# Expert blocks of 32 tokens in four column groups, with ten weight places, in a two-block transformer kernel

## The chip, the cores and the metric

The kernel runs on one core of a Trainium2 chip, as one program. The metric is the device time of one execution in microseconds; the kernel before was run three times.

## The reference

Two stacks of layers on 256 tokens of 1024 features, all in fp32. The first stack has two layers (latent attention, then a short convolution), each followed by a mixture of experts; the second has two layers of feed-forward, mixer, feed-forward. The part that matters here:

```python
def _hier_moe(h, w_group, b_group, w_expert, b_expert, w_gate, w_up, w_down):
    g_prob = softmax(h @ w_group)                       # 4 groups
    g_sel = argmax(g_prob + b_group)
    e_prob = softmax((h @ w_expert) of the chosen group) # 8 experts
    top_idx = top_k(e_prob + e_bias, 2)
    top_w = normalised e_prob[top_idx] * g_prob[g_sel]
    ...
    expert(x, e) = (silu(x @ w_gate[e]) * (x @ w_up[e])) @ w_down[e]
    return sum over the token's two experts of top_w * expert(token)
```

There are 32 experts. w_gate[e] and w_up[e] are 1024 x 512, w_down[e] is 512 x 1024, so each is one piece of 2 MB and an expert has 6 MB. Which tokens an expert gets is known only at run time.

## The kernel before

**Stages.** The engines run one list of stages: an opening, attention, norm, experts of layer 0, norm, convolution, norm, experts of layer 1, norm, and then a loop over the two layers of the second stack. The expert stage is the class `Moe`; it runs twice, on 256 tokens.

**Router.** TensorE forms the router's logits (L1480) and turns the tokens into rows (L1488), which ScalarE keeps (L1616) and writes to `f_rows` in HBM (L1619). VectorE picks each token's two experts in small steps. Tokens of an expert are put in blocks of `CAP` = 64. The number of blocks of an expert is one plus the number of multiples of `CAP` that its count exceeds (L1734 to L1737), and a token's block and place follow from its rank in the same way (L1748 to L1753). A table says for each block which tokens it has and with what weights (L1510, L1766 to L1770); it is done when `table_kept` is signalled. The first block number of each expert is in `FIRSTI`, and each engine reads its loop's limits from there (`range_of`). An expert has at least one block.

**One block**, in TensorE's order (`expert` in `Moe.pe`): gate (L1557) and up (L1558), 64 tokens as the stationary operand and 512 weight columns moving, gate in array columns 0 to 63 and up in 64 to 127, for eight slices of the 1024 features; then the next block's tokens are turned (`turn_block`, L1530); then the block before is combined (L1523); then the hidden rows are turned (L1574), and down (L1581, L1582) follows, again in two halves. An fp32 matmul shows as two records in the trace. Beside it ScalarE does SiLU (L1642), keeps the next tokens (L1633) and the down result (L1648); VectorE multiplies (L1780), keeps the turned hidden rows (L1783) and builds the combine matrix (L1787); GpSimd gathers the tokens of the block after the next from `f_rows` (L1820, L1823), as 128 half rows of 2 KB.

**Weights.** A piece of weights lives in a place of 16 KB a partition: six places in `ring` and three in `arena`, so nine, and experts e, e+1, e+2 hold three each (`AHEAD` = 3). SyncE issues all weight loads from one queue, in order. Ahead of the expert stage it issues the six loads into the ring as the stage before frees them, then three into the arena once the norm is done (L2911). When the table is there, a loop (L2947) issues for each expert e, in order, gate and up of expert e+3 when the last `hidden` of expert e is signalled, and down of e+3 when its last `down` is (L2944):

```python
for j, name in enumerate(("moe_w_gate", "moe_w_up", "moe_w_down")):
    freed = moe.hidden if j < 2 else moe.down
    sp.wait_ge(freed.sem, blocks)
```

Behind the loop it waits for the blocks of expert 30, and goes on with the next stage's loads (L2911). Such a load waits until the piece that was last in its ring place is used: for a piece of expert 31 that is the end of the last combine. Expert 31 has three ring places. In the second expert stage these are places 0, 1 and 2, which the first feed-forward loads want.

Other lines that are named: the conditioning matmuls of the opening (L452), the norm's sums (L724) and square root (L746), and the rounding of feed-forward weights on ScalarE (L2100).

Of the kernel before, what the change touches and what calls it, by code (L numbers as in the profile page):

```python
# [44 lines left out]
CAP = P // 2  # L45
# [17 lines left out]
AHEAD = (RING + EXTRA) // 3  # L63
# [125 lines left out]
def program(nc, xT, vec, base_c, mla_c, mix_c, w, out):  # L189
    ctx = ExitStack()  # L190
    with ctx:
# [69 lines left out]
        slot_in = [sig(f"slot_in{i}") for i in range(RING + EXTRA)]  # L261
# [1096 lines left out]
        class Moe:  # L1358
# [5 lines left out]
            def __init__(self, l, tokens, norm):  # L1364
# [36 lines left out]
                places = [(self.first + i) % RING for i in range(RING)] + [RING + i for i in range(EXTRA)]  # L1401
                for e in range(EXPERTS):

                    done = (self.down, 0) if e < EXPERTS - 1 else (self.combined, 2)
                    for j, (name, shape) in enumerate((("moe_w_gate", (2, 4 * FF)), ("moe_w_up", (2, 4 * FF)), ("moe_w_down", (1, FT * D)))):
                        plan(self.rows_of(name, w[name][l][e]), shape, done, places[3 * (e % AHEAD) + j])
# [29 lines left out]
                self.XG = take(512)  # L1436
                self.YS = take(512)

                rows_at = take.used()
                self.SG, self.H = take(FF), take(FF)  # L1440
                self.XB = take(512).rearrange("p (c a) -> p c a", c=4)
# [3 lines left out]
                assert rows_at + 2 * D == take.used() <= EXTRA_AT, (rows_at, take.used())  # L1445

            def rows_of(self, name, weight):

                if name == "moe_w_down":
                    return weight.rearrange("(o p c) n -> p o (c n)", o=1, p=P)  # L1450
                return weight.rearrange("(j p c) n -> p j (c n)", j=2, p=P)

            def weights(self, a, which):

                wv = slot(self.first + 3 * a + which)
                if which == 2:
                    return wv.rearrange("p (c n) -> p c n", c=FT)
                return wv.rearrange("p (j c n) -> p j c n", j=2, c=4)

            def arrived(self, eng, turn, a, which):  # L1460

                n = self.first + 3 * a + which
                eng.wait_ge(slot_in[place_of[n]].sem, turn * 16 + arrivals[n])
                eng.sem_inc(spare.sem, 1)

            ADDED = (0, 1, 4, 5, 2, 3, 6, 7)

            def combined_tile(self, k):

                return ps[:, (1, 4, 5, 6)[k // 2], k % 2 * TL:(k % 2 + 1) * TL]  # L1470

# [1606 lines left out]
```

## Time and profile before

| | |
|---|---|
| runs | 2464.44, 2465.23, 2462.46 us; median 2464.44 |
| profiled execution | 2464.74 us, its span 2462.9 us |
| mean granted TensorE clock | 0.980 of full speed |
| busy, share of the span | TensorE 95%, weight loads 66%, VectorE 46%, ScalarE 35%, GpSimd 4% |
| HBM | 677.87 MB read, 277 GB/s over the span |
| MB by weight loads of the expert stages | 192 loads of 2048 KB |

The two loops over the experts' blocks take 470 and 456 us of the span. Busy time of TensorE is that of records whose ends are modelled, so that it says little about how fast the records follow each other; for that their starts are read.

### The profile page before, as it was taken

To read this page: it belongs to the slowest core of one execution; us is meant where nothing else is said; L and a number is where in the kernel's file an instruction comes from. 1 tells how busy PE (TensorE), PEld (TensorE's weight loads), DVE (VectorE), ACT (ScalarE), POOL (GpSimd) and SP (SyncE) were. 2 spreads that over 40 slices of the span, in tenths; PEclk is the share of its full clock that TensorE was granted. 3 is DMA by queue.
4 is the path that set the end of the run, shared out by engine and by line. 5 is a ranking of instruction groups with operands and counts; after the bars stand their busy time and mean duration, and the time that the engine had idled before them with its cause. 6 is when DMAs were issued, how large, how long until landed. Compare 5 with 4: busy or idle time off the path is not lost.

```text
span 2462.9 us, 37675 instructions
## 1 busy us (share of the span) xinstructions
PE 2329.7 (95%) x13114; PEld 1621.6 (66%) x13117; DVE 1136.7 (46%) x2043; ACT 853.6 (35%) x1521; POOL 109.6 (4%) x180
## 2 busy tenths in 40 slices
PE   7999899999999989999999999998999999998997
PEld 3567444444447944444444688886888788886886
DVE  4676311111115641111111676776666766767666
ACT  2232111111114421111111555554554654554554
POOL 0000000000000000000000000000000000000000
PEclk8999899999999999999999999999999999999999
DMA  9974798999997549999998755435446456334552
GB/s 390 334 277 190 314 425 368 428 427 426 428 394 280 197 185 425 428 427 427 427 428 373 272 169 167 144 104 171 167 143 220 150 162 193 130 120 138 174 155 82
DMA packets 295807, 668.84 MB, mean 272 GB/s; under 512 B 10596, under 2 KB 205156, under 8 KB 254208
## 3 DMA queue, kind: packets, MB, share of 16 engines
q1 hardware_dynamic: 289440, 658.82, 69.4%
q0 software_dynamic: 5520, 4.23, 0.5%
q10 hardware_dynamic: 720, 4.13, 0.4%
q8 instruction: 76, 1.25, 0.2%
q14 instruction: 51, 0.42, 0.0%
HBM read 677.87 MB, written 3.15 MB: 277 GB/s over the span
## 4 chain that ended last, share of the span: by engine, by line
PE 87%; DVE 5%; DMA 3%; issue 2%; ACT 1%; SPq 1%; ACTq 0%; DVEq 0%; POOLq 0%; POOL 0%; PEldq 0%
PE ps L2120 19%; PE ps L1557 16%; PE ps L2125 10%; PE ps L1581 8%; PE ps L1523 5%; PE ps L2394 4%; PE ps L2559 2%; PE ps L1530 2%; DMA ring<-in_moe_w_up 2%; PE ps L1558 1%; PE ps L1923 1%; PE ps L1924 1%; PE ps L1925 1%; DVE arena L1783 1%; PE ps L1574 1%
## 5 line engine op out<-in xcount | busy, mean ns | idle before, releaser
L2120 PE MATMUL ps<-XS,WS 128*128 128x512 f32 x1408 | 500.4, 400 | 12.5 <-DVE XS L679 11.8
L2105 DVE TENSOR_TENSOR WS<-ring,WS 128x1024 fp32r<-128x1024 f32 (+1 forms) x276 | 329.5, 1194 | 229.8 <-ACT WS L2100 229.3
L2100 ACT CAST WS<-ring 128x1024 fp32r<-128x1024 f32 (+1 forms) x276 | 283.0, 1026 | 333.4 <-PE ps L2125 312.3
L2125 PE MATMUL ps<-XS,WS 128*128 128x256 f32 x1408 | 397.1, 282 | 0.0
L1780 DVE TENSOR_TENSOR arena<-arena,ps 64x512 f32<-64x512 f32 x65 | 44.8, 690 | 712.2 <-ACT arena L1642 712.2
L1557 PE MATMUL ps<-ring,arena 128*64 128x512 f32 x720 | 319.1, 597 | 5.1 <-issue 2.0
L2120 PEld LDWEIGHTS ps<-XS,WS 128*128 128x128 f32 x1408 | 265.7, 189 | 83.4 <-DVE XS L679 22.7
L1558 PE MATMUL ps<-ring,arena 128*64 128x512 f32 x720 | 319.3, 597 | 0.0
L2125 PEld LDWEIGHTS ps<-XS,WS 128*128 128x128 f32 x1408 | 268.6, 191 | 0.0
L1557 PEld LDWEIGHTS ps<-ring,arena 128*64 128x64 f32 x720 | 98.8, 138 | 192.6 <-issue 192.6
L2120 PE MATMUL ps<-HS,WS 128*128 128x512 f32 x616 | 216.7, 397 | 0.0
L2125 PE MATMUL ps<-HS,WS 128*128 128x256 f32 x704 | 197.7, 281 | 0.0
L1581 PE MATMUL ps<-ring,arena 128*64 128x512 f32 x360 | 162.8, 595 | 27.4 <-DVE arena L1783 27.4
L1648 ACT COPY arena<-ps 128x512 f32<-128x512 f32 x65 | 38.0, 585 | 390.9 <-PE ps L1582 390.9
L1642 ACT ACTIVATE arena<-ps 64x512 f32<-64x512 f32 x65 | 38.3, 589 | 367.2 <-PE ps L1558 367.2
L1582 PE MATMUL ps<-ring,arena 128*64 128x512 f32 x360 | 164.1, 599 | 0.0
L1557 PE MATMUL ps<-arena 128*64 128x512 f32 x320 | 140.6, 592 | 0.7 <-DMA arena<-in_moe_w_up 0.7
L1558 PE MATMUL ps<-arena 128*64 128x512 f32 x320 | 140.6, 593 | 0.0
L1523 PE MATMUL ps<-arena 64*128 64x256 f32 x1072 | 133.9, 389 | 1.8 <-ACT arena L1648 1.8
L2125 PEld LDWEIGHTS ps<-HS,WS 128*128 128x128 f32 x704 | 133.4, 190 | 0.1
L2120 PEld LDWEIGHTS ps<-HS,WS 128*128 128x128 f32 x616 | 115.6, 188 | 27.1
L1581 PEld LDWEIGHTS ps<-ring,arena 128*64 128x64 f32 x360 | 45.6, 136 | 101.5 <-issue 101.5
(361 smaller groups left out, 3668.7 us busy)
## 6 DMA issues: line engine op xcount, KB each, us to landing
ring<-in_ffn_w_gu SPq DMA_DIRECT2D x90, 1024.0 KB, 7.3
ring<-in_moe_w_gate SPq DMA_DIRECT2D x44, 2048.0 KB, 16.8
ring<-in_moe_w_up SPq DMA_DIRECT2D x44, 2048.0 KB, 21.5
ring<-in_moe_w_down SPq DMA_DIRECT2D x44, 2048.0 KB, 19.6
ring<-in_w_mod SPq DMA_DIRECT2D x24, 2048.0 KB, 10.2
ring<-in_ffn_w_down SPq DMA_DIRECT2D x32, 1408.0 KB, 6.5
arena<-in_moe_w_gate SPq DMA_DIRECT2D x20, 2048.0 KB, 17.2
arena<-in_moe_w_up SPq DMA_DIRECT2D x20, 2048.0 KB, 21.9
```

Of the source, the lines that this page charges most:

```text
L1523: mm = pe.matmul(self.combined_tile(4 * half + i), self.YS[rows, i * P:(i + 1) * P], self.COMBINE[rows, :], start=False, stop=last and i % ...
L1530: mm = pe.transpose(ps[:, 3, c * P:(c + 1) * P], by_four[:, c, :], IDENT)
L1557: pe.matmul(ps[0:CAP, 0, :], x, gate[:, j, c, :], start=k == 0, stop=k == KD - 1)
L1558: mm = pe.matmul(ps[CAP:P, 0, :], x, up[:, j, c, :], start=k == 0, stop=k == KD - 1)
L1581: pe.matmul(ps[0:CAP, 7, :], self.HB[:, c, :], down[:, c, 0:512], start=c == 0, stop=c == FT - 1)
L1582: mm = pe.matmul(ps[CAP:P, 7, :], self.HB[:, c, :], down[:, c, 512:D], start=c == 0, stop=c == FT - 1)
L2100: L.inc(L.eng.copy(self.parts(u)[0], source), self.w_high)
L2105: L.inc(L.eng.tensor_tensor(wl, self.unit(u)[1], high(wh), ALU.subtract), self.w_split)
L2120: L.eng.matmul(ps[:, bank, :].rearrange("p (j t) -> p j t", j=2), wh[:, i, :], moving[:, :, k, :], start=k == 0, stop=False)
L2125: mm = L.eng.matmul(ps[:, bank, 0:TL], wl[:, i, :], moving[:, 0, k, :], start=False, stop=k == total - 1)
L2394: mm = pe.matmul(out_ap, weights[:, k, :], XS[:, x, k, :], start=k == 0 and x == 0 and weights is high_part, stop=k == KD - 1 and weights ...
L2559: mm = pe.matmul(self.y_tile(m), weights[:, k - first, cols], YS[:, k, x, :], start=m % 2 == 0 and k == 0 and x == 0 and weights is high_part,
```

## The change

- `CAP` is 32. A block's gate and up are four products side by side in the array, each with 32 tokens stationary and 256 weight columns moving: gate in two halves, up in two halves, in array columns 0, 32, 64 and 96. Down is four quarters of 256 columns, and the combine uses the four groups of 32 rows. SiLU, the multiply and the copies work on 256 columns; the turned hidden rows are copied in two parts.
- The arithmetic for blocks and places uses one comparison with all multiples of `CAP` and a sum, in place of a step for each multiple. The count uses 2 columns in place of 128. The memset of the gathered rows is moved behind the rows' writes and ahead of the wait for the table.
- Tokens are gathered as 32 whole rows of 4 KB.
- All three kinds of weights are loaded as one row of 16 KB a partition (gate and up were two rows of 8 KB each).
- The tenth place is the memory `A` of the normed tokens, which is free once the tokens' rows are turned. Gate and up have four places each (two in the ring and two elsewhere), down has two, both in the ring. So gate and up of expert e+4 are loaded when expert e has used its own, down of e+2 when e has used its own. The last experts hold other ring places than before: expert 31 has one ring place only, its down.

```diff
-CAP = P // 2
+CAP = P // 4
+HALF_FF = FF // 2
-AHEAD = (RING + EXTRA) // 3
+AHEAD, DOWN_AHEAD = 4, 2
+A_PLACE = RING + EXTRA
...
+            if at == A_PLACE:
+                return A[:, :, :].rearrange("p k n -> p (k n)")
...
+                near = [(self.first + i) % RING for i in range(RING)]
+                far = [RING + i for i in range(EXTRA)] + [A_PLACE]
+                places = {"moe_w_gate": (near[0], near[3], far[0], far[2]), "moe_w_up": (near[1], near[4], far[1], far[3]),
+                          "moe_w_down": (near[2], near[5])}
...
                         for k in range(KD):
-                            c, j = k // 2, k % 2
-                            x = self.XB[:, c, j * CAP:(j + 1) * CAP]
-                            pe.matmul(ps[0:CAP, 0, :], x, gate[:, j, c, :], start=k == 0, stop=k == KD - 1)
-                            mm = pe.matmul(ps[CAP:P, 0, :], x, up[:, j, c, :], start=k == 0, stop=k == KD - 1)
+                            x = self.XB[:, k, :]
+                            for q in range(4):
+                                weight = (gate, up)[q // 2][:, k, q % 2 * HALF_FF:(q % 2 + 1) * HALF_FF]
+                                mm = pe.matmul(ps[self.lane_rows(q), 0, 0:HALF_FF], x, weight, start=k == 0, stop=k == KD - 1)
...
-                        pe.wait_ge(self.h_kept.sem, b + 1)
+                        pe.wait_ge(self.h_kept.sem, b * 2 + 2)
                         pe.sem_inc(spare.sem, 1)
                         for c in range(FT):
-                            pe.matmul(ps[0:CAP, 7, :], self.HB[:, c, :], down[:, c, 0:512], start=c == 0, stop=c == FT - 1)
-                            mm = pe.matmul(ps[CAP:P, 7, :], self.HB[:, c, :], down[:, c, 512:D], start=c == 0, stop=c == FT - 1)
+                            for q in range(4):
+                                mm = pe.matmul(ps[self.lane_rows(q), 7, 0:D // 4], self.HB[:, c, :],
+                                               down[:, c, q * (D // 4):(q + 1) * (D // 4)], start=c == 0, stop=c == FT - 1)
...
-                step(v.tensor_copy(self.CNT[0:EXPERTS, :], ps[0:EXPERTS, 6, 0:P]))
-                step(v.tensor_scalar(self.NBLK[0:EXPERTS, :], self.CNT[0:EXPERTS, :], float(CAP), 1.0, ALU.is_gt, ALU.add))
-                for r in range(2, -(-self.T // CAP)):
-                    step(v.scalar_tensor_tensor(out=self.NBLK[0:EXPERTS, :], in0=self.CNT[0:EXPERTS, :], scalar=float(r * CAP),
-                                                in1=self.NBLK[0:EXPERTS, :], op0=ALU.is_gt, op1=ALU.add))
+                over = self.CNT[0:EXPERTS, 0:limits]
+                step(v.tensor_tensor(over, self.LIMITS[0:EXPERTS], ps[0:EXPERTS, 6, 0:1].to_broadcast([EXPERTS, limits]), ALU.is_lt))
+                step(v.tensor_reduce(self.CNT[0:EXPERTS, limits:limits + 1], over, X, ALU.add))
+                step(v.tensor_scalar(self.NBLK[0:EXPERTS, :], ONES[0:EXPERTS, :], self.CNT[0:EXPERTS, limits:limits + 1], 1.0,
+                                     ALU.mult, ALU.add))
...
-                for i in range(EXTRA):
-                    load(n + i)
-                n += EXTRA
+                for e, j in ((2, 0), (2, 1), (3, 0)):
+                    load(moe.first + 3 * e + j)
+
+                sp.wait_ge(moe.rows_turned.sem, moe.rows_turned.base + moe.NT)
+                load(moe.first + 3 * 3 + 1)
...
+                    kinds = (("moe_w_gate", AHEAD, moe.hidden), ("moe_w_up", AHEAD, moe.hidden), ("moe_w_down", DOWN_AHEAD, moe.down))
+                    for j, (name, ahead, freed) in enumerate(kinds):
+                        if j == 2 or gate_too:
+                            sp.wait_ge(freed.sem, blocks)
+                            at = moe.first + 3 * a + j
+                            src = w[name][moe.l][bass.ds(e + ahead, 1)].rearrange("o (p c) n -> p o (c n)", p=P)
+                            sp.dma_start(loads[at][0][0], src).then_inc(slot_in[place_of[at]].sem, 16)
```

In SyncE's queue the loads ahead of the first expert stage's loop, and the loop's first expert, stand like this before (`gate`, `up` and `down` name the weights, the text ahead of the arrow the memory that is written; an ISA row is a wait):

```order
L2911 DMA arena<-in_moe_w_gate 128x2x2048
L2911 DMA arena<-in_moe_w_up 128x2x2048
L2911 DMA arena<-in_moe_w_down 128x4096
L2947 UNCONDITIONAL_BRANCH
L2947 ISA
L2931 TENSOR_LOAD arena
L2931 ISA x2
L2944 ISA
L2944 DMA ring<-in_moe_w_gate 128x2x2048
L2944 DMA ring<-in_moe_w_up 128x2x2048
L2944 DMA ring<-in_moe_w_down 128x4096
```

and with the change like this:

```order
L2925 DMA arena<-in_moe_w_gate 128x4096
L2925 DMA arena<-in_moe_w_up 128x4096
L2925 DMA arena<-in_moe_w_gate 128x4096
L2925 DMA A<-in_moe_w_up 128x4096
L2960 UNCONDITIONAL_BRANCH
L2960 ISA
L2947 TENSOR_LOAD arena
L2947 ISA x2
L2958 ISA
L2958 DMA ring<-in_moe_w_gate 128x4096
L2958 DMA ring<-in_moe_w_up 128x4096
L2958 ISA
```

The third piece ahead of the loop is now gate of expert 3, not down of expert 2, and a fourth goes to `A`; the down load follows behind a wait of its own.

On TensorE the end of a block's gate and up (L1557, L1558) and what follows it stand like this before:

```order
L1557 MATMUL ps<-ring,arena 64x512
L1558 MATMUL ps<-ring,arena 64x512
L1561 ISA
L1530 MATMUL ps<-BASE,arena 128x128 x4
L1523 MATMUL ps<-arena 128x256 x8
L1574 MATMUL ps<-BASE,arena 128x64 x4
```

and the whole block like this with the change:

```order
L1566 MATMUL ps<-ring,arena 32x256 x32
L1569 ISA
L1538 MATMUL ps<-BASE,arena 128x32 x8
L1531 MATMUL ps<-arena 128x256 x8
L1582 MATMUL ps<-BASE,arena 64x64 x4
L1467 ISA
L1587 ISA
L1591 MATMUL ps<-ring,arena 32x256 x16
```

The order of the block's parts is unchanged; gate and up are 32 matmuls of half the columns instead of 16, and down 16 instead of 8.

## Rows read from the trace of the kernel before

**Rows 1.** The page, part 5 (costliest groups; its heading gives the columns).
```profile
L1780 DVE TENSOR_TENSOR arena<-arena,ps 64x512 f32<-64x512 f32 x65 | 44.8, 690 | 712.2 <-ACT arena L1642 712.2
```
**Rows 2.** Stretches: us; busy time of PE, PEld, DVE, ACT, POOL; clock, DMA share, GB/s.
```profile
960.00:1320.00 360.00, 343.14 (x1822) 168.35 (x1820) 42.46 (x100) 54.84 (x84) 30.13 (x50) 1.00 1.01 427
282.00:288.00 6.00, 5.97 (x16) 2.10 (x18) 0.00 (x0) 1.28 (x1) 0.67 (x1) 0.55 0.05 10
396.00:400.00 4.00, 4.00 (x20) 1.55 (x18) 0.00 (x0) 0.58 (x1) 0.00 (x0) 1.00 0.64 269
400.00:404.00 4.00, 4.00 (x22) 1.68 (x20) 0.00 (x0) 0.00 (x0) 0.00 (x0) 1.00 0.01 4
404.00:408.00 4.00, 3.95 (x30) 2.69 (x26) 0.70 (x2) 1.18 (x2) 1.21 (x2) 1.00 0.44 123
```
**Rows 3.** Timeline, one block of the first expert stage: start, us taken, engine, instruction.
```profile
602.88 0.75 PE L1530 MATMUL ps<-BASE,arena 128*128 128x128 f32 x4
603.56 2.00 PE L1523 MATMUL ps<-arena 64*128 64x256 f32 x16
...
606.00 0.43 DVE L1783 COPY arena<-ps 128x256 f32<-128x256 f32 x1 [1.70 <-PE ps L1574]
...
606.58 0.61 PE L1581 MATMUL ps<-ring,arena 128*64 128x512 f32 x1 [0.61 <-DVE arena L1783]
...
610.03 0.59 PE L1557 MATMUL ps<-ring,arena 128*64 128x512 f32 x1
...
610.46 0.59 PE L1557 MATMUL ps<-ring,arena 128*64 128x512 f32 x1
...
617.03 0.75 PE L1530 MATMUL ps<-BASE,arena 128*128 128x128 f32 x4
```
**Rows 4.** Timeline, TensorE: the first gate record of either stage.
```profile
282.02 1.08 PE L1557 MATMUL ps<-ring,arena 128*64 128x512 f32 x1 [1.57 <-ACT arena L1633]
...
905.56 0.61 PE L1557 MATMUL ps<-ring,arena 128*64 128x512 f32 x1 [1.72 <-issue]
```
**Rows 5.** Timeline, SyncE's queue: gate loads in the expert loops.
```profile
291.97 0.40 SPq L2944 DMA_DIRECT2D ring<-in_moe_w_gate  x1
...
376.82 0.38 SPq L2944 DMA_DIRECT2D ring<-in_moe_w_gate  x1
...
405.11 0.37 SPq L2944 DMA_DIRECT2D ring<-in_moe_w_gate  x1
...
912.86 0.38 SPq L2944 DMA_DIRECT2D ring<-in_moe_w_gate  x1
```
**Rows 6.** Stretches in which the last weights of either stage arrive.
```profile
730.00:735.00 5.00, 4.39 (x32) 3.23 (x32) 1.70 (x4) 1.18 (x2) 1.20 (x2) 1.00 0.69 287
1345.00:1350.00 5.00, 4.76 (x24) 1.78 (x22) 0.00 (x0) 0.58 (x1) 0.00 (x0) 1.00 0.42 179
```
**Rows 7.** Timeline: the last down record of either stage, and what follows the second.
```profile
751.08 0.59 PE L1582 MATMUL ps<-ring,arena 128*64 128x512 f32 x1
...
1361.40 0.59 PE L1582 MATMUL ps<-ring,arena 128*64 128x512 f32 x1
...
1364.94 33.14 SPq L2911 DMA_DIRECT2D ring<-in_ffn_w_gu  x12
1365.07 3.72 PE L724 MATMUL ps<-A,BASE 128*128 128x256 f32 x16 [0.16 <-ACT A L703]
...
1373.01 1.99 ACT L2100 CAST WS<-ring 128x1024 fp32r<-128x1024 f32 x2 [5.25 <-DMA ring<-in_ffn_w_gu]
...
1376.31 0.42 ACT L746 ACTIVATE RS<-RS 128x256 f32<-128x256 f32 x1
```
**Rows 8.** Timeline, opening: weight loads of 128 rows by 32 columns.
```profile
22.37 0.13 PEld L452 LDWEIGHTS ps<-ring,arena 128*32 128x32 f32 x4 [0.30 <-issue]
...
22.80 0.13 PEld L452 LDWEIGHTS ps<-ring,arena 128*32 128x32 f32 x4 [0.30 <-issue]
```
**Rows 9.** Timeline, VectorE: a counting step of the router.
```profile
259.89 0.59 DVE L1737 SCALAR_TENSOR_TENSOR arena<-arena 32x128 f32<-32x128 f32 x2
```

More of the change, by code:

```diff
@@ L260, in program @@
         stages_done = sig("stages_done")
-        slot_in = [sig(f"slot_in{i}") for i in range(RING + EXTRA)]
+        slot_in = [sig(f"slot_in{i}") for i in range(A_PLACE + 1)]
         spare = sig("spare")
@@ L1444, in __init__, with rows_of, lane_rows @@
                 self.ROWS = [arena[:, rows_at + i * D:rows_at + (i + 1) * D] for i in range(2)]
[L1445 to L1451, printed above, removed]
+                assert rows_at + 2 * D <= take.used() <= EXTRA_AT, (rows_at, take.used())
+            def rows_of(self, weight):
+                return weight.rearrange("(o p c) n -> p o (c n)", o=1, p=P)
             def weights(self, a, which):
[L1455 to L1458, printed above, removed]
+                return slot(self.first + 3 * a + which).rearrange("p (c n) -> p c n", c=FT if which == 2 else KD)
             def arrived(self, eng, turn, a, which):
                 n = self.first + 3 * a + which
-                eng.wait_ge(slot_in[place_of[n]].sem, turn * 16 + arrivals[n])
+                per_turn = 16 * (AHEAD // DOWN_AHEAD if which == 2 else 1)
+                eng.wait_ge(slot_in[place_of[n]].sem, turn * per_turn + arrivals[n])
                 eng.sem_inc(spare.sem, 1)
-            ADDED = (0, 1, 4, 5, 2, 3, 6, 7)
+            ADDED = tuple(range(KD))
             def combined_tile(self, k):
                 return ps[:, (1, 4, 5, 6)[k // 2], k % 2 * TL:(k % 2 + 1) * TL]
+            def lane_rows(self, q):
+                return slice(q * CAP, (q + 1) * CAP)
             def pe(self, L):
@@ L1513, in pe @@
                 L.inc(mm, self.table)
[L1515 to L1516 removed]
+                by_eight = self.XG[0:CAP].rearrange("p (n c) -> p c n", c=KD)
+                hidden_by_four = self.H[0:2 * CAP].rearrange("p (n c) -> p c n", c=FT)
                 def combine(last=False):
[L1520 to L1526 removed]
+                    for i in range(2):
+                        for q in range(4):
+                            rows = self.lane_rows(q)
+                            mm = pe.matmul(self.combined_tile(2 * q + i), self.YS[rows, i * P:(i + 1) * P], self.COMBINE[rows, :],
+                                           start=False, stop=last and i == 1)
+                            if last and i == 1 and q % 2 == 1:
+                                L.inc(mm, self.combined)
                 def turn_block():
[L1529 to L1530 removed]
+                    for c in range(KD):
+                        mm = pe.transpose(ps[:, 3, c * CAP:(c + 1) * CAP], by_eight[:, c, :], IDENT[0:CAP, 0:CAP])
                     mm.then_inc(self.block_turned.sem, 1)
@@ L1747, in dve @@
                     pick(self.BLK[c], row(self.FIRST[:, 0:EXPERTS], EXPERTS), self.O32[c], EXPERTS)
-                    step(v.tensor_scalar(self.QUOT[c], self.RANK[c], float(CAP), None, ALU.is_ge))
-                    for r in range(2, -(-self.T // CAP)):
-                        step(v.scalar_tensor_tensor(out=self.QUOT[c], in0=self.RANK[c], scalar=float(r * CAP), in1=self.QUOT[c],
-                                                    op0=ALU.is_ge, op1=ALU.add))
+                    over = self.TMP[:, :, 0:limits]
+                    step(v.tensor_tensor(over, lanes(self.RANK[c], limits), row(self.LIMITS, limits), ALU.is_ge))
+                    step(v.tensor_reduce(self.QUOT[c][:, :, 0], over, X, ALU.add))
                     step(v.tensor_tensor(self.BLK[c], self.BLK[c], self.QUOT[c], ALU.add))
```

84 lines of the change are left out of this document (35 added, 49 removed).

## The prediction

> **What bounds the kernel now.** I read the page first, then each expert stage by stretches, then one block in order of time, then SyncE's queue, and last the two ends of a stage. The page counts 65 trips of the block loop (x65), 33 in the first expert stage and 32 in the second [rows 1]. The stretches show two limits side by side: from 960 to 1320 us TensorE is busy 343 of 360 us at clock 1.00, and the DMA engines are busy all the time (share 1.01) at 427 GB/s [rows 2]. Which of the two ends last is read from the block. From one block's token transposes (602.88) to the next's (617.03) it is 14.15 us: 16 pairs of gate and up records, 6.86 us at 0.4286 a pair; 3.70 us from the transposes to the first down matmul; 8 pairs of down, 3.43 us; a seam of 0.15 [rows 3]. So TensorE needs 14.14 us a block, and the two stages take 282.0 to 751.7 and 905.6 to 1362.0 [rows 3, 4, 7].
>
> The DMA side: an expert's three pieces are 2.097 MB each. In the second stage the first load in the loop is issued at 912.86 [rows 5], its first bytes come some 2 us later, and the last of 87 pieces is in at 1347.1, since the stretch 1345 to 1350 still moves data for 42% of its time [rows 6]: 432.2 / 87 = 4.97 us a piece, 14.9 an expert. The first stage gives the same: 294.0 to 733.4, less 7.7 us without traffic between 396 and 408 (36%, 99% and 56% of three stretches of 4 us), is 431.7 / 87 = 4.96 [rows 2, 5, 6]. That gap is the one expert with two blocks: one expert's gate load is issued at 376.82, the next one's only at 405.11. So the stages are almost balanced: TensorE paces them at 14.14, DMA could do no better than 14.9 and lives on nine pieces loaded beforehand, which are used up just at the end.
>
> **The change, part by part.**
>
> *How many blocks.* I worked the router out from the reference with its inputs. Blocks of 64 give 33 and 32, as the trace has. Blocks of 32 give 36 and 34: in the first layer experts 0, 7 and 25 get 34, 74 and 38 tokens (2, 3 and 2 blocks), in the second experts 4 and 27 get 60 and 48 (2 each). 70 blocks instead of 65.
>
> *One block.* Gate and up are now four column groups of 32 with 256 columns each. Whether four groups run together is shown at the start of this kernel, where a conditioning matmul uses exactly that form: four weight loads of 128x32 begin together, and the next four 0.43 us later (22.37, 22.80), with 512 columns each [rows 8]. A group of four records so takes what a pair takes now, and with 256 columns half of it, 0.214. Gate and up have 16 such groups, 3.43 us, and down 8, 1.72. The middle part stays near 3.7: eight transposes of 32 rows in place of four of 128 (bounds: 0.68 us as now, to twice that, taken 1.2), the combine with four row groups instead of two (2.00 us as now, to half, taken 1.1), SiLU and multiply on half the columns (hidden below both), and two copies in place of one of 0.43 before down (between none and 0.5 more, taken 0.3) [rows 3]. Sum: 3.43 + 3.7 + 1.72 + 0.1 = 8.95 us a block, bounds 8.3 and 10. An expert with one block then needs 9 us of TensorE and 14.9 of DMA: **the stage becomes DMA bound**, and only 1 us of TensorE speed in many shows.
>
> *The loads.* They can be spared nothing in bytes. Rows of 16 KB for gate and up: down has such rows already in the same stream and the stream stands at 427 GB/s; bounds 0 and 2% faster, taken 0.3%, 4.95 us a piece. The tenth place takes one more piece before the loop, so 86 remain: 425.7 us a stage. The Trainium skill (DMA: Bandwidth & Descriptors, "Where 436 GB/s comes from") puts the ceiling at 435 GB/s; at that rate a piece would take 4.82 us and the two stages would give 22 us more. No row here holds more than 427 over a long stretch.
>
> *First stage.* The router's shorter counting (two steps in place of the 0.59 us of L1737 and two more, twice again for the ranks, a count of 2 columns instead of 128) and a memset taken off the path give 1.5 us (0 to 3) [rows 9], so the loop starts at 280.5. The first block runs at half clock as now (0.55 from 282 to 288) [rows 2], 3 us extra. Expert 0 has two blocks, so its gate is free at 280.5 + 6.4 + 5.5 + 3.5 = 295.9; 2.3 us later data flow, at 298.2; plus 425.7 is 723.9. Expert 7 with three blocks holds its places until the four deep gate and up queue is nearly dry: 3 us. Last come the down pieces of experts 29, 30 and 31, 4.95 us apart, and behind the first of them two whole blocks and one down: 19.6 - 9.9 = 9.7 us after the last byte, taken 11 since TensorE restarts cold after a wait. End 737.9, against 751.7: **13.8 us saved**.
>
> *Second stage.* Loop start 905.6 - 1.5 = 904.1 [rows 4]; gate free after 3.4 us, data at 909.8; plus 425.7, 1 us for the two double experts, 11 of tail: 1347.5, against 1362.0: **14.5 us saved**.
>
> *Behind the stages.* The last combine is halved and its copy shorter: 0.6 us each, 1.2. The first feed-forward loads now wait for the last combine (issued 1364.94), so ScalarE's cast waits for them until 1373.01, and the square root of the norm behind it starts at 1376.31 [rows 7]. With the new places the first two go to places freed by experts 28 and 29, and are issued when expert 30 is done, some 8 us before the loop ends. The cast can then follow the norm's sums, which end at 1368.8 (1365.07 + 3.72): **4.1 us**. For the conv weights the same is worth nothing, they are there in time now.
>
> *What I cost at nothing.* The new load into the normed tokens' memory waits for the row transposes; the engines still work off the nine before it, or are early anyway. The token gather is 32 rows of 4 KB in place of 128 of 2 KB, beside a stream that is full as before; its cover is the whole block, now 9 us instead of 14, and it shows only in the five experts with several blocks. SyncE now stands in a down wait ahead of the next expert's gate load; that load is needed three experts later.
>
> Sum: 13.8 + 14.5 + 1.2 + 4.1 = 33.6. The profiled execution took 2464.74 us (span 2462.9), 0.3 above the median of 2464.44. 2464.7 - 33.6 = **2431 us**.
>
> **The rivals.**
> - *Half the gain* (18%). A block takes 11 to 12, not 9: TensorE waits 5 us in every expert and comes back at half clock, or four groups are fed more slowly than four 512-column groups. One more us in a block costs some 5.5 us in the first stage (start 1.5, expert 7 two, tail two) and 3.5 in the second. At 11.2 us a block that is 20 us: 2451. For it: behind the wait for the first gather the clock stood at 0.55 [rows 2].
> - *Slower* (9%). One mechanism: the same restart at half clock doubles gate, up and down, or four groups run as two pairs, and a block costs 6.86 + 3.7 + 3.43 = 14.0 and a seam, 14.2. Then TensorE bounds again, with 70 blocks where there were 65: 994 against 919, less the 9 us at starts and ends: 2531. It decides from (919 + 9) / 70 = 13.3 us a block. Against it: [rows 8], and that a TensorE which is that busy keeps clock 1.00 [rows 2]. The Trainium skill (TensorE: Matmul & The Clock Gate, "HAM oscillation — how this bites in real kernels") describes just this, a short burst after each DMA wait that starts cold every time. By that rule each expert starts cold; the trace agrees at 282 to 288 [rows 2].
> - *Faster DMA* (5%). The longer rows bring the 2% of the upper bound, 4.87 us a piece in place of 4.95 over 172 pieces: 14 us, 2417.
> - *DMA is hidden anyway* (5%). If the stages hung on something that the two rates don't show, such as SyncE's issue (its waits are all for TensorE in the loop), only the 5 us at the ends would come: 2459.
>
> **How the numbers follow.** The forecast has 63%; its own range is 2423 to 2440 (block 8.3 to 10, piece 4.90 to 4.97, router 0 to 3). The range for 8 in 10 takes in most of the half gain and a little of the faster DMA: 2417 to 2452. 0.2% is 5 us, about what a measurement of this kernel can tell. Slower by more: the 9%. Within: 4%, from the last rival and the upper end of the first. Faster: 87%.
>
> **What would show it.** Blocks x70; records of gate and up four at a time every 0.214 us; a block of 9 us where an expert has several; TensorE waiting for the down piece in most experts, about 5 us each; DMA share 1.0 from some 298 and 910 us to within 11 us of the loops' ends, 730 to 740 and 1342 to 1350; the cast of the first feed-forward weights without a DMA wait. It would be wrong if records pair up at 0.43, if the granted clock stays near 0.5 with a block above 13 us, or if a piece takes other than 4.9 to 5.0 us.

## The result, and the profile after

The changed kernel takes 2471.56 us (median of 10 runs, 2465.55 to 2476.93); the kernel before, run beside it, 2464.89. The ratio is 1.0033, 95% interval 1.0022 to 1.0043: slower by 6.7 us, where 33 us less was forecast. Its profiled execution took 2476.93 us (span 2474.8) and is the slowest of the ten. It has 5 us over the median, and they lie behind the expert stages: from the first feed-forward matmul to the end of the span it takes 1087.9 us, the kernel before 1082.7.

The page, part 5 (columns as in [rows 1]), answers to [rows 1] and shows what TensorE now waits for:

```profile
L1591 PE MATMUL ps<-ring,arena 128*32 128x256 f32 x2240 | 213.5, 546 | 267.0 <-DMA ring<-in_moe_w_down 248.8
...
L1791 DVE TENSOR_TENSOR arena<-arena,ps 64x256 f32<-64x256 f32 x70 | 29.6, 423 | 731.7 <-ACT arena L1652 731.7
```

70 blocks, as forecast. TensorE stands still for 267 us ahead of the down products (L1591), 249 of them waiting for a down piece: the stages are DMA bound, as forecast. One block cold and the next waiting, and two blocks in a row later on (timeline of TensorE, columns as in [rows 3]):

```profile
1027.70 3.64 PE L1591 MATMUL ps<-ring,arena 128*32 128x256 f32 x32 [4.00 <-DMA ring<-in_moe_w_down]
1031.08 4.25 PE L1566 MATMUL ps<-ring,arena 128*32 128x256 f32 x64
...
1043.65 2.79 PE L1591 MATMUL ps<-ring,arena 128*32 128x256 f32 x24 [6.00 <-DMA ring<-in_moe_w_down]
...
1342.01 1.93 PE L1591 MATMUL ps<-ring,arena 128*32 128x256 f32 x32 [0.78 <-DVE arena L1797]
1344.82 3.66 PE L1566 MATMUL ps<-ring,arena 128*32 128x256 f32 x64 [0.87 <-issue]
...
1350.35 0.46 PE L1582 MATMUL ps<-BASE,arena 64*64 64x64 f32 x4
1351.74 1.93 PE L1591 MATMUL ps<-ring,arena 128*32 128x256 f32 x32 [0.94 <-DVE arena L1797]
```

Gate and up take 3.66 us and down 1.93, four column groups side by side; a block takes 1351.74 - 1342.01 = 9.7 us. Behind a wait down takes 3.64: the granted clock was 0.50 from 1028 to 1031. The stretches (columns as in [rows 2]) show the DMA side:

```profile
1000.00:1290.00 290.00, 187.06 (x2351) 112.83 (x2350) 30.01 (x95) 27.68 (x62) 21.03 (x38) 0.75 1.01 423
...
404.00:408.00 4.00, 4.00 (x81) 2.90 (x76) 0.00 (x0) 0.37 (x1) 0.00 (x0) 1.00 0.22 93
...
730.00:735.00 5.00, 1.40 (x16) 0.83 (x20) 0.00 (x0) 0.00 (x0) 0.00 (x0) 0.50 0.52 218
735.00:740.00 5.00, 5.00 (x64) 2.69 (x60) 0.00 (x0) 0.37 (x1) 0.00 (x0) 0.62 0.43 111
1323.00:1330.00 7.00, 7.00 (x99) 4.46 (x95) 0.42 (x1) 1.04 (x3) 0.08 (x1) 0.80 0.50 194
1350.00:1355.00 5.00, 3.18 (x53) 1.81 (x50) 1.16 (x4) 0.37 (x1) 0.93 (x1) 1.00 0.57 179
...
1040.00:1042.00 2.00, 0.00 (x0) 0.00 (x0) 0.00 (x0) 0.00 (x0) 0.00 (x0) 0.50 0.97 412
1042.00:1044.00 2.00, 0.35 (x4) 0.23 (x8) 0.00 (x0) 0.00 (x0) 0.00 (x0) 0.50 1.05 311
1044.00:1046.00 2.00, 2.00 (x24) 1.13 (x20) 0.00 (x0) 0.00 (x0) 0.00 (x0) 0.50 0.99 418
```

The engines are busy all the time (1.01), yet move 423 GB/s where the kernel before had 427 [rows 2]. At 1042 to 1044 they are as busy as ever and move 311: a dip in the rate, not a gap. And near either loop's end they go idle and start again, which they did not before. The starts and ends (TensorE, then ScalarE) answer to [rows 4, 7]:

```profile
278.65 1.94 PE L1566 MATMUL ps<-ring,arena 128*32 128x256 f32 x16 [1.63 <-issue]
...
754.12 1.93 PE L1591 MATMUL ps<-ring,arena 128*32 128x256 f32 x32 [0.78 <-DVE arena L1797]
...
910.97 1.29 PE L1566 MATMUL ps<-ring,arena 128*32 128x256 f32 x20 [0.61 <-ACT arena L1643]
...
1370.82 1.93 PE L1591 MATMUL ps<-ring,arena 128*32 128x256 f32 x32 [0.78 <-DVE arena L1797]
...
1379.49 1.99 ACT L2114 CAST WS<-ring 128x1024 fp32r<-128x1024 f32 x2 [1.16 <-PEq L325]
...
1386.94 0.80 PE L2134 MATMUL ps<-XS,WS 128*128 128x512 f32 x1
```

From the first of these gate records to the end of the last down product the loops take 477.4 us (before 469.7) and 461.8 (before 456.4). From the second one's end to the first feed-forward matmul it is 14.2 us, 18.2 before.

### The profile page after: what moved, and what is told of

Its sections match the earlier page's. It is cut to its first block, busy times and chain, and to the rows that moved or that the text cites. A ratio compares the mean times of both kernels' runs of the same rounds, so it can differ in the third digit from the quotient of the medians.

```text
span 2474.8 us, 46063 instructions
## 1 busy us (share of the span) xinstructions
PE 2091.8 (85%) x17124; PEld 1588.0 (64%) x17125; DVE 1136.8 (46%) x2129; ACT 814.6 (33%) x1534; POOL 109.2 (4%) x190
## 4 chain that ended last, share of the span: by engine, by line
PE 63%; DMA 27%; DVE 5%; issue 3%; ACT 1%; SPq 1%; POOLq 0%; DVEq 0%; ACTq 0%; POOL 0%; PEldq 0%
DMA ring<-in_moe_w_down 25%; PE ps L2134 19%; PE ps L2139 10%; PE ps L1591 5%; PE ps L2408 4%; PE ps L1566 3%; PE ps L2573 2%; PE ps L1937 1%; PE ps L1939 1%; PE ps L1938 1%; DMA arena<-f_rows,arena 1%; PE ps L1098 1%; PE ps L1531 1%; PE ps L2449 1%; PE ps L1538 1%
## 5 line engine op out<-in xcount | busy, mean ns | idle before, releaser
L1591 PE MATMUL ps<-ring,arena 128*32 128x256 f32 x2240 | 213.5, 546 | 267.0 <-DMA ring<-in_moe_w_down 248.8
L2139 PE MATMUL ps<-XS,WS 128*128 128x256 f32 x1408 | 397.1, 282 | 0.0
L1791 DVE TENSOR_TENSOR arena<-arena,ps 64x256 f32<-64x256 f32 x70 | 29.6, 423 | 731.7 <-ACT arena L1652 731.7
L2134 PEld LDWEIGHTS ps<-XS,WS 128*128 128x128 f32 x1408 | 265.9, 189 | 83.9 <-DVE XS L683 19.3
L1591 PEld LDWEIGHTS ps<-ring,arena 128*32 128x32 f32 x2240 | 100.3, 148 | 338.7 <-issue 330.3
L2139 PEld LDWEIGHTS ps<-XS,WS 128*128 128x128 f32 x1408 | 267.8, 190 | 0.2 <-issue 0.2
L1658 ACT COPY arena<-ps 128x256 f32<-128x256 f32 x70 | 26.0, 372 | 549.3 <-PE ps L1591 549.3
L1566 PE MATMUL ps<-ring,arena 128*32 128x256 f32 x2240 | 140.5, 406 | 13.6 <-issue 13.0
L1566 PE MATMUL ps<-arena 128*32 128x256 f32 x1632 | 140.3, 404 | 9.5 <-issue 9.5
L1566 PEld LDWEIGHTS ps<-ring,arena 128*32 128x32 f32 x2240 | 84.9, 118 | 73.9 <-issue 42.7
L1566 PEld LDWEIGHTS ps<-arena 128*32 128x32 f32 x1632 | 83.0, 118 | 66.9 <-issue 33.7
L2408 PE MATMUL ps<-XS,WS 128*128 128x256 f32 x768 | 100.4, 288 | 0.0
L1652 ACT ACTIVATE arena<-ps 64x256 f32<-64x256 f32 x70 | 26.3, 375 | 222.3 <-PE ps L1566 222.3
L2408 PEld LDWEIGHTS ps<-XS,WS 128*128 128x128 f32 x768 | 94.8, 191 | 3.1 <-issue 2.3
L1531 PE MATMUL ps<-arena 32*128 32x256 f32 x1152 | 94.8, 398 | 1.4 <-ACT arena L1658 1.4
```

Of the source, the lines that this page charges most:

```text
L1531: mm = pe.matmul(self.combined_tile(2 * q + i), self.YS[rows, i * P:(i + 1) * P], self.COMBINE[rows, :], start=False, stop=last and i == 1)
L1566: mm = pe.matmul(ps[self.lane_rows(q), 0, 0:HALF_FF], x, weight, start=k == 0, stop=k == KD - 1)
L1591: mm = pe.matmul(ps[self.lane_rows(q), 7, 0:D // 4], self.HB[:, c, :], down[:, c, q * (D // 4):(q + 1) * (D // 4)], start=c == 0, stop=c = ...
L1652: act.activation(self.SG[2 * CAP:P], ps[0:2 * CAP, 0, 0:HALF_FF], ACT.Silu).then_inc(self.gated.sem, 1)
L1658: act.copy(self.YS, ps[:, 7, 0:D // 4]).then_inc(self.y_kept.sem, 1)
L1791: v.tensor_tensor(self.H[0:2 * CAP], self.SG[2 * CAP:P], ps[2 * CAP:P, 0, 0:HALF_FF], ALU.mult)\
```

## The experiments

### Rows, depth, places

The first suspicion was what the change did to the loads: 16 KB rows for gate and up (theory R, rows), and two places for down (theory D, depth). In e1 gate and up are two rows of 8 KB:

```diff
-        plan(self.rows_of(w[name][l][e]), (1, SLOT), done, ...)
+        plan(self.rows_of(name, w[name][l][e]), (1, SLOT) if name == "moe_w_down" else (2, 4 * FF), done, ...)
```

> The changed kernel, with gate and up loaded as two rows of 8 KB a partition again (down stays one row of 16 KB), nothing else changed. Theory D (depth): the loss lies in the two places for down: its load is issued only when the down products two experts earlier are done, so that the last pieces come one behind the other with the DMA engines idle between them, and an expert with several blocks holds the stream up. It expects no change here: 2468 to 2475, against 2471.6. Theory R (rows): the loss lies in the rate. The trace of the changed kernel has 420 to 426 GB/s in steady stretches where the one before had 427, with 16 KB packets of over 700 ns in the dips beside 611 ns elsewhere. It expects 427 GB/s again, and 8 to 15 us less: 2457 to 2463.

2472.83 us, ratio 1.0038 (1.0024 to 1.0053), and 421 GB/s from 1000 to 1290 us: the rate doesn't come back, and theory R falls. Here and below the ratio is to the kernel before as it ran beside the same experiment.

e2 goes back to nine places, three for each kind of weights:

```diff
-AHEAD, DOWN_AHEAD = 4, 2
+AHEAD, DOWN_AHEAD = 3, 3
-                for e, j in ((2, 0), (2, 1), (3, 0)):
+                for e, j in ((2, 0), (2, 1), (2, 2)):
```

> The changed kernel with the places of the kernel before: nine, three deep for gate, up and down alike, no tenth in A; blocks of 32 and 16 KB rows stay. Theory D: the last down piece is issued three experts before its use, the DMA idle time at either stage's end (7.8 and 6.8 us) goes, and behind the last byte only one expert's down is left, some 5 us where it was 11 to 15: 10 to 13 us less a stage, less 5 us a stage for the piece that isn't loaded ahead, and 4 us for the first feed-forward loads that wait again: 2455 to 2465. Theory R: the rate stays at 424, one more piece to load a stage and the late feed-forward loads: 2480 to 2486.

2465.11 us, 1.0012 (0.9996 to 1.0028). The DMA engines no longer go idle ahead of the last pieces, so D is right in its mechanism, and yet the kernel is only where the one before is. The stretches show two things beside it: 423 GB/s as in the changed kernel, and at the end of the second loop a DMA share that falls to nothing over some 13 us.

```profile
1000.00:1290.00 290.00, 189.30 (x2356) 115.43 (x2356) 30.04 (x95) 30.25 (x64) 21.02 (x38) 0.83 1.01 423
...
1344.00:1348.00 4.00, 3.22 (x53) 2.42 (x56) 1.58 (x5) 0.37 (x1) 1.11 (x2) 1.00 0.57 242
1348.00:1352.00 4.00, 0.59 (x12) 0.11 (x4) 0.00 (x0) 0.37 (x1) 0.00 (x0) 1.00 0.31 131
1352.00:1356.00 4.00, 3.52 (x36) 1.94 (x40) 0.00 (x0) 0.00 (x0) 0.00 (x0) 0.57 0.15 55
```

A piece is there when all 16 engines have signalled it (its semaphore is waited for in steps of 16). A share that falls so slowly says that some engines finish long before others; the trace doesn't tell them apart.

e3 is e1 and e2 at once:

> Both at once: nine places three deep, gate and up in rows of 8 KB; of the change only the blocks of 32 in column groups (and the router's arithmetic and the gather) are left. Theory D: as with three deep alone, 2455 to 2465. Theory R: as with 8 KB rows alone plus the 14 us that the shallower gate and up cost, 2471 to 2477. If both hold, the sum of the two: 2443 to 2453. If neither holds, the block's form or its cold starts cost what is lost, and the time stays above 2470.

2467.96 us, 1.0012 (0.9997 to 1.0027): no more than e2. e4 gives the kernel before the new places alone (blocks of 64, 8 KB rows):

> The kernel before (blocks of 64 in two halves, 8 KB rows for gate and up) with the new places alone: gate and up four deep, down two, the tenth in A. Theory D: TensorE needs 14.15 us an expert, a down piece issued behind the down products of two experts earlier has 28 us to arrive and took 26 in the changed kernel, so it just about arrives, but the last pieces and the expert with two blocks cost: 2462 to 2475. Theory R: the places cost nothing and bring the 4 us of the early feed-forward loads: 2459 to 2463.

2467.36 us, 1.0009 (0.9997 to 1.0022): no difference that can be told. By its trace the places do cost the old blocks something, 473.6 and 463.2 us for the loops in place of 469.7 and 456.4, and give back 3.8 us behind the second. Neither theory explains the 33 us that were forecast and didn't come.

### The gather

The dips have a date: they come each time GpSimd's gather lands. I sorted the weight packets of 1000 to 1290 us by whether a packet of the gather was within 0.7 us. The table has the mean time of 16 KB of them, and the share of all weight packets over 0.65 us per 16 KB:

```
kernel                       near the gather   elsewhere   over 0.65 us
before                            0.619 us       0.618         0.2%
places alone (e4)                 0.619          0.618         0.3%
changed                           0.670          0.612         6.6%
8 KB rows (e1)                    0.683          0.619         5.6%
three deep (e2)                   0.672          0.613         6.7%
quarter rows (e5)                 0.615          0.611         0.3%
half rows (e6)                    0.677          0.616        11.9%
half rows spread (e9)             0.613          0.611         0.0%
```

Every kernel with whole rows in 32 partitions has slow packets, whatever its weight rows and places; the two with the old gather don't. In the changed kernel all 487 slow ones start within 0.7 us of the start of a packet of the gather. The mean near the gather moves between 0.66 and 0.68 with how "near" is counted, the last column doesn't. In e5 the tokens are gathered as 128 quarter rows:

```diff
-                    for c in range(KD):
-                        mm = pe.transpose(ps[:, 3, c * CAP:(c + 1) * CAP], by_eight[:, c, :], IDENT[0:CAP, 0:CAP])
+                    for c in range(2):
+                        mm = pe.transpose(ps[:, 3, c * P:(c + 1) * P], by_two[:, c, :], IDENT)
...
-                    g.indirect_dma_start(out=self.XG[0:CAP], out_offset=None, in_=f_rows,
-                                         in_offset=bass.IndirectOffsetOnAxis(ap=self.IDXG[0:CAP], axis=0),
+                    g.indirect_dma_start(out=self.XG, out_offset=None, in_=f_rows.rearrange("t (j d) -> (t j) d", j=4),
+                                         in_offset=bass.IndirectOffsetOnAxis(ap=self.IDXG, axis=0),
```

> The changed kernel, whose tokens are gathered as 128 quarter rows of 1 KB over all partitions in place of 32 whole rows of 4 KB in partitions 0 to 31 (f_rows is written with the features permuted to fit; two transposes of 128x128 in place of eight of 32x128). The new theory G (gather): within 0.7 us of a packet of the gather, a 16 KB weight packet takes 0.670 us in the changed kernel and 0.612 elsewhere, 7 to 12% of all packets are over 0.65 us; in the kernel before, whose gather is 128 half rows, 0.619 and 0.618, and 0.3%. The gather clogs the stream, 1.5 to 2.5% of it or 7 to 10 us a stage. It expects slow packets under 1%, and 12 to 20 us less than 2471.6: 2452 to 2460. Theory D (two places for down): the depth is untouched, only the shorter transposes show: 2468 to 2473. A third, T (TensorE reads four streams from SBUF at once and slows the writes): slow packets stay as they are, no change.

**2438.50 us** (4 runs, 2437.47 to 2439.93), ratio 0.9895 (0.9876 to 0.9913): 33 us less than the changed kernel, more than theory G (the gather clogs the stream) asked. The rate is back, through the landing of a gather too (the last three rows; its DMA is issued at 1044.46):

```profile
1000.00:1290.00 290.00, 182.15 (x2259) 102.55 (x2259) 31.03 (x99) 26.41 (x61) 23.92 (x39) 0.76 1.01 430
...
1046.00:1048.00 2.00, 0.00 (x0) 0.00 (x0) 0.00 (x0) 0.00 (x0) 0.00 (x0) 0.50 0.99 426
1048.00:1050.00 2.00, 0.00 (x0) 0.00 (x0) 0.00 (x0) 0.00 (x0) 0.00 (x0) 0.50 1.02 430
1050.00:1052.00 2.00, 1.42 (x16) 0.85 (x20) 0.00 (x0) 0.00 (x0) 0.00 (x0) 0.50 1.02 434
```

What in the gather does it? e6 has 64 half rows of 2 KB in partitions 0 to 63:

```diff
+                    g.indirect_dma_start(out=self.XG[0:2 * CAP], out_offset=None, in_=f_rows.rearrange("t (j d) -> (t j) d", j=2),
```

> The same with 64 half rows of 2 KB in partitions 0 to 63. It asks what in the gather clogs. If it is the length of a row or its number of requests, half rows are as good as in the kernel before, and the slow packets go as with quarters. If it is the few partitions that all bytes go to (an expert has 16 tokens on average, so whole rows fill partitions 0 to 15, half rows 0 to 15 and 32 to 47, quarters also 64 to 79 and 96 to 111), then it depends on where halves land: by the number of partitions alone the slow packets halve, 3 to 4%, and the time is 2462 to 2466. By the Trainium skill (SBUF — State Buffer, "Door 1: The DMA port swizzle") a partition and the one 32 above share a port, so that half rows would help nothing against whole ones: 7 to 12% slow, about 2471.

2470.14 us, 1.0018 (1.0008 to 1.0029), and 11.9% slow packets: twice the partitions and half the length help nothing. Nearly half of the slow packets (402 of 879) come in one stretch, 1040 to 1060 us, most of them away from a gather; what slowed them is not known, and without that stretch the share is 6.9%, like that of whole rows.

```profile
1000.00:1290.00 290.00, 174.74 (x2247) 102.84 (x2243) 29.87 (x95) 27.34 (x61) 21.83 (x38) 0.76 1.01 420
```

e9 differs from e6 in where the second halves go, partitions 64 to 95. For that the gather has 128 indices in place of 64, those of the other places out of bounds, and the transposes are 128 wide:

```diff
-    half = (np.arange(P)[:, None] // CAP - 2).astype(f)
+    part = np.arange(P)[:, None] // CAP
+    half = np.where(part % 2 == 0, part // 2 - 2, 8192).astype(f)
```

> The kernel of the half rows again, with one difference: the second half of a token's row goes to partitions 64 to 95 in place of 32 to 63 (the places between get no row). Rows, their length and their number are the same. If the ports decide (the pages' rule that partitions p and p+32 share one and p+64 has another), slow packets go below 1% as with quarter rows, and the time is 2438 to 2445. If it was something else in the whole and half rows (their length, or how few requests there are), it stays at 2465 to 2475 with 11% slow packets.

2443.98 us, 0.9919 (0.9897 to 0.9941), no slow packets:

```profile
1000.00:1290.00 290.00, 186.97 (x2316) 108.49 (x2308) 31.43 (x100) 31.41 (x63) 24.10 (x40) 0.77 1.01 430
```

The same bytes in the same rows, moved up by 32 partitions, are worth 26 us. That e9's gather has more packets (some 76, with 48 in e6) is not what helps: that of e5 has 48 too and slows nothing. The Trainium skill (SBUF — State Buffer, "Door 1: The DMA port swizzle") has the rule: bits 2 to 4 and bit 6 of the partition's number choose one of 16 ports, bit 5 none. By that rule the 16 tokens that an expert has on average fill 4 ports as whole rows and as halves at 0 and 32, and 8 as halves at 0 and 64 (as in the kernel before) or as quarters; the trace agrees with it in all five gathers: those with 4 ports slow the packets beside them, the others don't. What is shown is that the partitions decide. That they do it through the ports is the page's account; which DMA engines carry the rows may change with the partitions too, and the trace doesn't name the engine of a packet. Why e9 stays 5 us behind e5 was not tried (2.5 of them lie in the first loop); its turned tokens are copied as 512 columns in place of 256.

### With the gather mended

> Quarter rows and the nine places three deep of the kernel before together; of the change the blocks of 32, the 16 KB rows and the router's arithmetic are left. If G and D both hold, their gains add: the three-deep kernel took 2465.1, less 12 to 20: 2445 to 2453, which beats the kernel before (2464) by 0.4 to 0.8%. If G is wrong it takes 2463 to 2467.

The edits of e2 and e5 together: 2439.13 us, 0.9902 (0.9882 to 0.9921), the same as e5. With a clean stream the depth is worth something and loses it again: the first loop is 4.6 us shorter than in e5 (no gap at its expert with three blocks, none at its end), the second no shorter, and the late feed-forward loads cost 3.3 (17.4 us from the second loop's end to the first feed-forward matmul, 14.2 in e5). The DMA engines now stop sooner and closer together than in e2, within some 9 us:

```profile
1316.00:1320.00 4.00, 1.93 (x32) 1.13 (x32) 0.70 (x3) 0.37 (x1) 0.33 (x1) 1.00 0.84 356
1320.00:1324.00 4.00, 0.97 (x12) 0.60 (x16) 0.00 (x0) 0.00 (x0) 0.00 (x0) 0.71 0.47 199
1324.00:1328.00 4.00, 4.00 (x44) 2.08 (x40) 0.00 (x0) 0.00 (x0) 0.00 (x0) 0.50 0.17 74
```

e8 also moves expert 31 into the arena:

```diff
+                places = {"moe_w_gate": (near[0], far[0], near[3]), "moe_w_up": (near[1], far[1], near[4]),
+                          "moe_w_down": (near[2], far[2], near[5])}
```

> The one before, with expert 31's three pieces in the arena, so that the first feed-forward loads find their ring places free when expert 30 is done, as in the changed kernel. There the end of the loop to the first feed-forward matmul took 14.2 us, and 18.2 in the kernel before. It expects 3 to 5 us less than the one before.

2434.26 us, 0.9878 (0.9858 to 0.9898): 4.9 less, as expected. e10 is e8 with 8 KB rows (the edit of e1):

> The fastest kernel so far (quarter rows, three deep, expert 31 in the arena: 2434.3), with gate and up as two rows of 8 KB again. With the gather out of the way the rows' own worth is seen: the median 16 KB packet takes 611 ns, and two 8 KB ones 618, 1.1% more on two pieces of three, 3 us a stage. It expects 5 to 8 us more: 2439 to 2442. If packets of other sizes only shift the time inside a full stream, no change.

2438.02 us, 0.9889 (0.9872 to 0.9906), 3.8 more than e8 at nearly the same time of the kernel before (2465.5, 2464.6), where 5 to 8 were expected. Its rate is 427 GB/s, that of e8 429. The two intervals overlap, so by the times alone it isn't shown; the traces are clearer. 16 KB take 0.618 us and 0.611 (medians), and the loops 459.5 and 450.4 us in place of 456.7 and 447.5, some 2.9 a stage. e11 uses all ten places in turn:

```diff
+                places = near[0:3] + far[0:3] + near[3:6] + far[3:4]
...
+                        plan(self.rows_of(w[name][l][e]), (1, SLOT), done, places[(3 * e + j) % 10])
```

> Quarter rows, and all ten places used in turn by all 96 pieces (gate, up, down, gate, ... ; the loop's body is ten experts), so that each piece is loaded ten ahead of its use. Against the fastest so far (nine places, 2434.3) one more piece is there before either loop: 4.9 us a stage, if the DMA stream alone sets the end: 2423 to 2428. If the longer loop body (three times the instructions) makes the engines wait for their code, or if the stream doesn't set the end, it takes 2434 or more.

**2433.15 us**, 0.9875 (0.9858 to 0.9891): the lowest median of all, but only 1.1 us below e8, which is no difference, where 6 to 11 were expected. Its loops are as long as e8's (456.6 and 448.2 us, 456.7 and 447.5). They have one piece less to load, and lose it to idle DMA engines: in the second loop, up to the last packet, the idle time of the engines (mean of the 16) is 15.8 us, in e8 10.2. Why they idle was not settled; the loop's body is three times as long. e12 is e8 kept at full clock:

```diff
+                    keep_busy(L, 4, 0)
                     for which in range(2):
                         self.arrived(pe, turn, a, which)
```

> The kernel of quarter rows, three deep, expert 31 in the arena (2434.3), with four matmuls on constants ahead of every expert's wait for its gate and up, which keep TensorE busy for about half of the 5 us that it waits there. Theory C (cold): an expert's gate and up take 5.1 to 6.3 us behind such a wait and 3.66 where the clock stayed up; if that counts in the time, it can do so only where no wait follows: behind the last piece of a stage, some 2 us each, and behind the experts with several blocks. It expects 2429 to 2432. If the DMA stream covers all of it, or the added matmuls cost the multi-block experts what the last one gains, it stays at 2433 to 2436.

2438.53 us, 0.9901 (0.9874 to 0.9929), 4.3 more than e8. The clock is 0.97 from 1000 to 1290 us, where e8 has 0.86, and the rate is 430 in both: in the middle of a stage a warm TensorE wins nothing.

```profile
1000.00:1290.00 290.00, 237.79 (x2636) 132.45 (x2635) 33.06 (x105) 33.81 (x71) 25.37 (x42) 0.97 1.01 430
```

At the ends of the stages it is another matter. The first gate and up of the first stage and the last of the second, in e8 and then in e12 (with the added matmuls, L339):

```profile
277.41 5.33 PE L1567 MATMUL ps<-ring,arena 128*32 128x256 f32 x64 [1.99 <-issue]
...
1323.39 6.27 PE L1567 MATMUL ps<-arena 128*32 128x256 f32 x64 [4.97 <-DMA arena<-in_moe_w_up]
```

```profile
276.46 6.41 PE L339 MATMUL ps<-BASE 128*128 128x512 f32 x8 [1.34 <-issue]
...
282.80 3.66 PE L1568 MATMUL ps<-ring,arena 128*32 128x256 f32 x64
...
1330.53 3.66 PE L1568 MATMUL ps<-arena 128*32 128x256 f32 x64 [1.00 <-DMA arena<-in_moe_w_up]
```

The last expert of the second stage takes 2.6 us less, as theory C expected for the end of a stage (the last expert of the first stage starts cold in both, 5.35 us). The added matmuls cost more than that: they stand ahead of each stage's first expert too, whose weights are there already, and hold up its gate, by 5.4 us in the first stage (1.7 of them come back) and 2.7 in the second. A kernel that warms all experts but the first was not tried.

## Why the prediction was wrong

The forecast (2431, range 2417 to 2452) was missed on the slow side, and none of its rivals is what happened. The stretches of e5, which is the changed kernel with another gather, show which steps held. us, from the first gate record to the end of the last down, each relative to its own start:

```
                                   before   forecast   changed    e5
first stage's loop                  469.7     457.4      477.4   460.7
between the loops                   153.9     151.8      154.9   153.1
second stage's loop                 456.4     443.4      461.8   446.9
loop's end to feed-forward           18.2      13.5       14.2    14.2
```

```profile
278.48 3.77 PE L1567 MATMUL ps<-ring,arena 128*32 128x256 f32 x40 [1.99 <-issue]
...
737.28 1.93 PE L1592 MATMUL ps<-ring,arena 128*32 128x256 f32 x32 [0.78 <-DVE arena L1799]
...
892.28 3.01 PE L1567 MATMUL ps<-ring,arena 128*32 128x256 f32 x52 [1.93 <-issue]
...
1337.27 1.93 PE L1592 MATMUL ps<-ring,arena 128*32 128x256 f32 x32 [0.78 <-DVE arena L1799]
...
1353.38 0.80 PE L2136 MATMUL ps<-XS,WS 128*128 128x512 f32 x1
```

- **The step that failed** is in "What I cost at nothing": "The token gather is 32 rows of 4 KB in place of 128 of 2 KB, beside a stream that is full as before; its cover is the whole block". The cover hides how long the gather takes. It doesn't hide what the gather does to the stream beside it, and the stream had just become the bound. With the gather in quarters the kernel takes 33.1 us less (2471.56 - 2438.50): 16.7 in the first loop, 14.9 in the second, by the table. A small part of that may be e5's shorter transposes, since blocks without a wait take from 9.1 us there and from 9.5 in the changed kernel; e6 and e9, where they don't get shorter, differ by 26.2. In the second loop, from one down load to the next it is 15.31 us in the changed kernel (17 experts, 1016.72 to 1276.93) and 14.88 in e5 (19 experts, 994.86 to 1277.59): 0.43 us in each of 30 experts is 13 of the 14.9. The packets themselves give less, 5.03 us a piece (mean of the 16 engines) against 4.92, which is 10 us in 86 pieces; the rest is more idle time of the engines, most of it in the last 90 us of the loop (9.2 against 5.1). That the slowest engine falls further behind would join the two numbers; it isn't shown. I had costed a transfer by its size and its latency, and not by where it lands.
- *How many blocks*: right, 70. *One block*: four groups side by side, right; 9.7 us, not 8.95 (down 1.93 for 1.72, gate and up 3.66 for 3.43, the middle and the seams 4.1 for 3.8), inside the bounds. In e5 it is 9.1 to 9.8.
- *The kernel before*: the last piece of its second loop was read as in at 1347.1, from a stretch that moves data for 42% of its time. The share is a mean of 16 engines; its packets go on to 1351.7, some 9 us after the first engine falls idle. The rate per piece that was worked out from it comes out right as a mean, but the last byte comes later than a mean says.
- *DMA bound*: right; 249 us of waits for down, about 3.6 a block where 5 an expert was named.
- *The loads*: three pieces at 4.95 us are 14.85; e5 has 14.88, the changed kernel 15.31, so 5.10 a piece, outside the bounds.
- *Expert 7*: taken 3 us. The engines are idle for most of 404 to 410 in the changed kernel, and they are half idle for another 4 us at the double expert 25 (678 to 682, share 0.54).
- *The tail*: mis-sized. "Last come the down pieces ... 4.95 us apart" took them as issued back to back. Each is issued only when down of two experts earlier is done, so the last experts go at TensorE's pace, one down in 9.1 to 9.8 us, with the DMA engines half idle (1323 to 1330, 1350 to 1355). In e5 the same happens (share 0.72 from 1294 to 1299 and 0.62 from 1319 to 1323), and its loops are 3.3 and 3.5 us above the forecast at the forecast's rate. The 11 us behind the last byte were about right (9.8 and 10.9 in e5); what was short lies ahead of it: in the second loop the last byte comes 436.1 us after the start, 432.4 forecast.
- *Router*: 1.5 us forecast ahead of the first loop, which starts 3.4 us earlier (278.65 for 282.02), above the bound of 3. Between the loops, with the halved last combine, 2.1 us forecast; in e5 it is 0.8, and in the changed kernel it takes 1.0 more than before.
- *Behind the stages*: 4.1 and 0.6 forecast, 4.0 measured, the cast without a DMA wait.
- *The rival of the restart*: in two blocks of three it does restart at half clock (44 of 70 down products take about twice the time of the others), which comes near to the rule of the Trainium skill (TensorE: Matmul & The Clock Gate, "HAM oscillation — how this bites in real kernels"), by which each burst behind a DMA wait starts cold. By e12 this costs nothing where the next piece is waited for anyway, and 2.6 us at the end of the second stage. A block of 14 us, on which the slower rival stood, never came: 9.7 warm, and some 11 cold were under the wait for the next piece.

e5 at 2438.5 lies inside the forecast's range: 7 us above 2431, of which the table has 3.3 + 1.3 + 3.5 + 0.7 = 8.8, less the 2 us by which the first loop starts earlier than forecast. That it comes so near is partly luck: errors of either sign cancel in it.

## What to carry to other kernels

When a change makes a stage DMA bound, go again through every small transfer that runs beside the bulk one, also those that were hidden before, and ask to which partitions it writes. Spread a gather over both halves of the partitions, 0 to 63 and 64 to 127, here as 128 quarter rows; moving a part of it up by 32 alone did nothing. The cost doesn't show as a wait for the gather but as a lower rate at full DMA share. And if a rate falls while the share stays 1.0, sort the packets by what else was in flight.

## What the runs showed of the hardware

- A gather of some 60 KB (16 rows of 4 KB) into partitions 0 to 31, or 0 to 63, slows the weight packets near it from 0.61 us to 0.67 or 0.68 on average; with its second half at 64 in place of 32 (e9) it slows none.
- A packet of 16 KB takes 0.611 us, two of 8 KB take 0.618 (medians): 429 and 427 GB/s over 290 us (e8, e10).
- At the end of a stage the share of the 16 DMA engines falls to nothing over some 9 us with a clean stream (e7, 1318 to 1327; the kernel before, 1343 to 1352), 13 with the clogged one (e2, 1344 to 1357). The last byte comes later than the mean rate says.
- Gate and up of a block take 3.66 us warm and 6.27 behind a wait of 5 us for their weights (e8). Where the next piece is waited for anyway the difference costs nothing; in the last expert of a stage it does.
- Four column groups of 32x256 fp32 follow each other at 0.22 us a group of four records, half of what four of 512 columns take [rows 8].
